# A two-layer streaming-encoder trunk: a rebuilt prologue, three pairs of weight slabs multiplied tile by tile, the low weight halves made in quarters, rotations in two banks

## The reference

```python
mod = (c @ w + b)                      # adaLN: 1024 x 3072 matrix, per layer and sub-layer
shift, scale, gate = split(mod, 3)
u = x * (1 + scale) + shift
# mixer
proj = u @ w_in                        # split into a, g (conv group), q, k, v (attention group)
h = silu(layer_norm(causal_dwconv(a * sigmoid(g), conv_w (31 taps), conv_b)))
q, k = partial_rotary(q, cos, sin), partial_rotary(k, cos, sin)   # angles = positions * inv_freq
o = swa_sink_attention(q, k, v, sinks) # chunks of 64 frames, window 128
y = concat([h, o]) @ w_out
x = layer_norm(DN_ALPHA * x + (1 + gate) * y)
# MLP, with its own adaLN
val, g = split(u @ w_up)               # D_FF = 2816
y = (val * silu(causal_dwconv(g, 3 taps))) @ w_down
x = layer_norm(DN_ALPHA * x + (1 + gate) * y)
```

## Time and profile before

| | |
|---|---|
| median of three runs | 2279.89 us |
| the profiled execution: its own time | 2280.07 us |
| its span, first to last instruction | 2278.3 us |
| TensorE busy | 2131.2 us (94%) |
| VectorE, ScalarE, GpSimd busy | 1255.8, 1008.8, 1230.0 us |
| mean granted TensorE clock | 0.971 |
| w_lo on GpSimd (L1506) | 392 instructions, 858.2 us |
| waits of TensorE, largest | 26.6 us for first_acc, 19.7 us for the parameter rows |

### The profile page before, as it was taken

The page is one execution under the profiler, slowest core; times in us unless marked ns, Lnnn a source line. Parts: engine busy times, 40 slices in busy tenths (PEclk is TensorE's granted clock), DMA queues, the critical chain, the costliest instruction groups (busy, mean ns, idle before and its releaser), DMA issues.

```text
span 2278.3 us, 25841 instructions
## 1 busy us (share of the span) xinstructions
PE 2131.2 (94%) x9491; PEld 1717.9 (75%) x9491; DVE 1255.8 (55%) x1924; ACT 1008.8 (44%) x1758; POOL 1230.0 (54%) x702
## 2 busy tenths in 40 slices
...
GB/s 247 133 137 131 37 163 96 98 124 141 114 127 102 110 120 134 134 152 113 88 73 94 102 91 98 95 96 84 85 80 88 100 83 102 111 94 129 93 95 72
DMA packets 414058, 248.72 MB, mean 109 GB/s; under 512 B 44293, under 2 KB 389101, under 8 KB 412909
## 3 DMA queue, kind: packets, MB, share of 16 engines
...
q10 hardware_dynamic: 2221, 0.55, 0.1%
...
## 4 chain that ended last, share of the span: by engine, by line
PE 74%; DVE 9%; POOL 7%; issue 5%; ACT 3%; DMA 1%; ACTq 0%; DVEq 0%; POOLq 0%
PE fg L699 23%; PE fg L701 23%; PE fg L700 23%; POOL w_lo L1506 2%; POOL ada_acc L1550 2%; DVE bank_c L1209 1%; DVE st L1325 1%; PE bank_s L767 1%; DVE probs L1329 1%; POOL ssum L1557 1%; DMA rows<-in_ffn_conv_w_dram 1%; DVE first_acc L1150 1%; ACT tmp L885 1%; POOL q L1535 0%; PE bank_t L776 0%
## 5 line engine op out<-in xcount | busy, mean ns | idle before, releaser
L1506 POOL TENSOR_TENSOR w_lo<-raw,w_hi 128x1024 fp32r<-128x1024 f32 (+2 forms) x392 | 858.2, 2189 | 932.3 <-ACT w_hi L877 932.1
L699 PE MATMUL fg<-u_hi,w_hi 128*128 128x512 f32 x2112 | 856.0, 405 | 14.6 <-DVE u_lo L1189 6.3
L700 PE MATMUL fg<-u_lo,w_hi 128*128 128x512 f32 x2112 | 829.2, 393 | 0.0
L701 PE MATMUL fg<-u_hi,w_lo 128*128 128x512 f32 x2112 | 828.9, 392 | 0.0
L877 ACT ACTIVATE w_hi<-raw 128x1024 fp32r<-128x1024 f32 (+2 forms) x392 | 379.4, 968 | 409.3 <-PE fg L701 349.2
L699 PEld LDWEIGHTS fg<-u_hi,w_hi 128*128 128x128 f32 x2112 | 401.2, 190 | 120.9 <-issue 22.9
L700 PEld LDWEIGHTS fg<-u_lo,w_hi 128*128 128x128 f32 x2112 | 401.1, 190 | 89.8 <-issue 10.3
L701 PEld LDWEIGHTS fg<-u_hi,w_lo 128*128 128x128 f32 x2112 | 400.4, 190 | 86.0
L1430 DVE SCALAR_TENSOR_TENSOR x<-fg,mod,x 128x512 f32<-128x512 f32 x160 | 119.8, 749 | 347.7 <-PE fg L701 347.7
L1209 DVE SCALAR_TENSOR_TENSOR bank_c<-glu,par,bank_c 128x512 f32<-128x512 f32 x448 | 306.1, 748 | 0.0
L699 PE MATMUL fg<-h_hi,w_hi 128*128 128x512 f32 x704 | 281.7, 400 | 0.2 <-DVE h_lo L1463 0.2
...
## 6 DMA issues: line engine op xcount, KB each, us to landing
raw<-in_w_up_dram SPq DMA_DIRECT2D x176, 512.0 KB, 3.8
...
```

The source lines that it names most:

```text
L699: pe.matmul(out[:], hi[:, k, :], rhi, start=k == order[0], stop=False)
L700: pe.matmul(out[:], hi[:, k, :], rlo, start=False, stop=False)
L701: ins = pe.matmul(out[:], lo[:, k, :], rhi, start=False, stop=k == order[-1])
L1506: pool.tensor_tensor(w_lo[n % NRAW][:, 0:nk, :], raw[n % NRAW][:, 0:nk, :], w_hi[n % NHI][:, 0:nk, :].bitcast(F32), ALU.subtract).then_inc ...
```

## The change

1. **Prologue.** The first adaLN matrix comes in eight pieces of 512 rows by 512 columns (four column chunks, two pieces each), each with a buffer of its own, laid between the loads of x. VectorE adds up chunk by chunk, TensorE sums a chunk over partitions as soon as it is complete, straight into `bank_s`, from which VectorE folds `gain` and `bias`. The angles go to GpSimd, the conv weights' rows and the sinks are loaded later, ScalarE alone empties the banks of x, and slabs 0 and 1 are both split before. VectorE makes its own copy of the modulated input (`first_tmp`) while ScalarE writes `u_hi` from x.
2. **Pairs.** Slabs 0 and 1, 22 and 23, 36 and 37 are multiplied together: for each tile of the input the three matmuls of one slab, then the three of the other. Both have to be ready at the start.
3. **Quarters.** GpSimd makes `w_lo` two tiles (256 columns) at a time.
4. **Rotations** alternate between `bank_t` and `bank_s`.
5. **Plan.** `u_lo` of block 1 moves from VectorE to GpSimd and costs the planner nothing, so that taps move to earlier slots; the eight squares of the first residual norm stand in one slot, its other steps one slot earlier, and its last step (`xo`, ScalarE) in slots 38 to 45; adaLN chunks 11 to 23 come later.

```diff
-    fixed = {... "xl": 7, "il": 10, "xt": 7, ...}
+    fixed = {... "xl": 7, "il": 0, "xt": 7, ...}
+PAIRS = (0, POS["o", 0, 0, 0], FIRST_UP)
-    x_norm(0, wait + 9, 4, wait + 12, wait + 13, 4)
+    x_norm(0, wait + 9, 8, wait + 11, wait + 12, 4)
+    for k in range(DT):
+        put(wait + 17 + k, "xo", 0, k)
...
@@ SyncE
             def load_first(k):
-                if k >= 3:
-                    sp.wait_ge(first_add, k - 2)
-                sp.dma_start(first_ada[k % 3][:], a["w_ada_mix"][0, k * P:(k + 1) * P, 0:2 * D]).then_inc(in_first[k % 3], 16)
+                rows, cols = slice(k % 2 * D // 2, (k % 2 + 1) * D // 2), slice(k // 2 * T, (k // 2 + 1) * T)
+                sp.dma_start(first_ada[k][:], a["w_ada_mix"][0, rows, cols].rearrange("(k p) n -> p k n", p=P)).then_inc(in_first[k], 16)
-            for t in range(TB):
-                load_x(t)
-            for k in range(6):
-                load_first(k)
-            load_w(0)
-            load_first(6)
-            load_first(7)
+            load_x(0)
+            load_first(0)
+            for t in range(1, TB):
+                load_x(t)
+                load_first(t)
+            load_first(4)
+            load_w(0)
+            load_first(5)
+            load_first(6)
+            load_first(7)
+            load_w(1)
+            load_rows(rows2, rows3)
...
@@ TensorE
+            def slabs(*ns):
...
+                    for n in ns:
+                        out, hi, lo = fg[BANK[n]], w_hi[n % NHI], w_lo[n % NRAW]
+                        pe.matmul(out[:], hi[:, k, :], rhi, start=k == order[0], stop=False)
+                        pe.matmul(out[:], hi[:, k, :], rlo, start=False, stop=False)
+                        ins = pe.matmul(out[:], lo[:, k, :], rhi, start=False, stop=k == order[-1])
...
-                take("t", rope_add, (QT + 2) * mi + (j + 1 if j < QT else QT + 2))
-                pe.matmul(bank_t[:], rot, q[mi][:, :, j, :] if j < QT else k_raw,
+                take("ts"[j % 2], rope_add, (QT + 2) * mi + (j + 1 if j < QT else QT + 2))
+                pe.matmul((bank_t, bank_s)[j % 2][:], rot, q[mi][:, :, j, :] if j < QT else k_raw,
...
+            for c in range(CHUNKS_BEFORE):
+                pe.wait_ge(first_add, DT * (c + 1))
+                for i in range(c * TB, (c + 1) * TB):
+                    ins = pe.matmul(bank_s[:, i:i + 1], first_acc[:, i * P:(i + 1) * P], ones_1[:, 0:1], start=True, stop=True)
...
@@ VectorE
+            for c in range(CHUNKS_BEFORE):
+                for k in range(DT):
+                    add_first(c, k)
+            fold("ss", 0)
...
+                first_tmp(k)
+                if k:
+                    first_lo(k - 1)
...
@@ GpSimd
-                pool.tensor_tensor(w_lo[n % NRAW][:, 0:nk, :], raw[n % NRAW][:, 0:nk, :], w_hi[n % NHI][:, 0:nk, :].bitcast(F32),
-                                   ALU.subtract).then_inc(lo_ready, 1)
+                for k in range(0, nk, LO_TILES):
+                    ks = slice(k, min(k + LO_TILES, nk))
+                    ins = pool.tensor_tensor(w_lo[n % NRAW][:, ks, :], raw[n % NRAW][:, ks, :], w_hi[n % NHI][:, ks, :].bitcast(F32),
+                                             ALU.subtract)
+                ins.then_inc(lo_ready, 1)
...
+            def second_lo(k):
+                pool.wait_ge(ihi, DT + k + 1)
+                pool.tensor_tensor(u_lo[1][:, k, :], tmp[:, k % 2, :], u_hi[1][:, k, :].bitcast(F32), ALU.subtract).then_inc(ilo, 1)
...
+            angles()
+            pool.wait_ge(first_add, DT * CHUNKS_BEFORE)
+            for n in range(2):
+                split_lo(n)
```

More of the change, by code:

```diff
@@ L63 @@
     _n += _c
-IN_CONST = 2 + len(ROWS1) + 2 * DEPTH
+IN_CONST = 1 + len(ROWS1)
 def conv_slabs(l, b, tiles):
```

346 lines of the change are left out of this document (183 added, 163 removed).

## The result

| | before | after |
|---|---|---|
| median, us | 2278.94 (2276.76 to 2280.75, 4 runs) | 2229.89 (2227.96 to 2231.71, 4 runs) |
| ratio | | 0.9781, 95% interval 0.9768 to 0.9793 |
| profiled execution, us | 2280.07, span 2278.3 | 2230.16, span 2228.4 |
| GpSimd busy, us | 1230.0 (54%) | 1422.8 (64%) |
| VectorE busy, us | 1255.8 | 1183.0 |

The change wins 50 us, and 2230 was forecast. The total hides that it is made of other parts than I had said. The first view to read is the windows by stage, cut at the starts of the slabs that bound the stages (core, then per engine busy us and count, granted clock, DMA share, GB/s); they answer to the earlier trace rows.

The account below looks back on a forecast made before the run. TensorE was taken as nearly always busy from 700 us, so gains lay in the first 430 us: 24.5 + 5.5 + 5.4 + 10.5 + 6.5 = 52.4 off 2280.07, taken as 50: 2230 us, 8-in-10 range 2214 to 2252.

Parts of the forecast that it names:

- A: Prologue and first pair: first matmul at 45 us, slab 2 at 59 instead of 83.2, gain 24 us (14 to 27).
- B: Slabs 2 to 13: GpSimd becomes the bound, first scores at 150 to 154; 24.5 us gained together with the prologue.
- G: The rest of the kernel: extra GpSimd pieces against shorter VectorE waits, counted 0, from -4 to +4 us.
- E: First residual norm and third pair, 337 to 393 us: earlier scale and filled wait, gain 10.5 us (6 to 13).
- F: Rotations of block 1, 393 to 428 us: two banks leave one wait of 2.6 us, gain 6.5 (3 to 8).
- D: Behind slab 21: taps moved ahead leave only the last sum, gain 5.4 us; second pair booked at 0.
- C: Slots 14 to 21: quarters shorten VectorE's waits for GpSimd, gain 5.5 us, bounds 0 and 10.
- rival (3): Quarters free VectorE more widely, in slots 14 to 21 and beats behind 428 us: 8 us more, about 2221; chance 0.13.
- 1 (0.9 us a piece): GpSimd swallows more: w_lo pieces cost 0.9 us instead of 0.69, 14 to 16 us less gain, 2245; chance 0.2.
- 2 (transfers): Prologue bound by its transfers at 300 GB/s, last piece 8 us later, 2239 to 2242 us; chance 0.12.
- 4: Slower than before: w_lo pieces have a floor of about 1.2 us, some 70 slots lose, 2290 to 2350; chance 0.03.
- 5: A new wait, such as pairs needing both w_lo, eats the first stage: same time within 0.2%; chance 0.02.

Follow-up runs that it names:

- e3_nopairs: The changed kernel with no slab pairs; 2221.38 us, ratio 0.9742 to the kernel before.
- e1_whole: The changed kernel with w_lo in one whole 128x1024 piece per slab again; 2235.53 us, ratio 0.9805 to the kernel before.
- e10_both: The changed kernel with only the first pair, the cosine product ahead of w_lo (mixers 1 to 3), whole w_lo in slabs 0-16 and 110-140; 2205.21 us.
- e12_ulo: e10_both with the eight u_lo of block 1 computed on VectorE again instead of GpSimd; 2210.32 us, ratio 0.9687 to the kernel before.
- e4_onebank: The changed kernel with all rotations in bank_t, as before; 2243.01 us, ratio 0.9836 to the kernel before.
- e6_bank: The changed kernel, all three pairs, with banks 1 and 2 exchanged from slab 36 on; 2222.26 us, ratio 0.9753 to the kernel before.
- e2_quarters: The kernel before with one edit, w_lo in pieces of two weight tiles; 2267.71 us, ratio 0.9945 to the kernel before.
- e7_product: The changed kernel with the first pair alone and GpSimd's cosine product ahead of w_lo for mixers 1 to 3; 2210.78 us, ratio 0.9699 to before.
- e9_adaplaces: The kernel before with only the change's places of the adaLN quarters and their folds; 2278.41 us, ratio 0.9992 to the kernel before.

## Why the prediction was right, step by step

The total is right, and by luck: A and B gave 3.6 us more than forecast and G 12, E and F 13.7 less, D and the slabs from 22 to 33 4.4 less. A and C hold in the main, B and D in part; E, F and G miss.

**A, 24 forecast, 25.6 measured.** VectorE's last seven adds ended at 37.0, the last sums took 1.86 us, the two folds 0.17 each, the eight pieces of `w_lo` 6.51 for my 5.5 and five VectorE instructions of 0.55 between them, 8.3 in all, and the first matmul came at 43.9 for 45 (answers to the earlier trace rows):

```profile
31.51 5.54 DVE L1173 SCALAR_TENSOR_TENSOR first_acc<-first_ada,ccol,first_acc 128x512 f32<-128x512 f32 x7
37.11 1.86 PE L846 MATMUL bank_s<-const,first_acc 128*128 128x1 f32 x8 [4.17 <-DVE first_acc L1173]
37.19 6.51 POOL L1533 TENSOR_TENSOR w_lo<-raw,w_hi 128x256 fp32r<-128x256 f32 x8 [3.12 <-issue]
43.91 0.77 PE L727 MATMUL fg<-u_hi,w_hi 128*128 128x512 f32 x1 [4.20 <-POOL w_lo L1533]
```

The last piece of the matrix landed at 33.4 us for my 33. The middle of the prologue moved 373 GB/s (16 to 28 us) for my 390, but VectorE waited for no piece behind 27.9 us, so its adds set the end and not the transfers. The 28 steps of the angles took 18.4 us on GpSimd (15.7 to 34.1), not my 12: about 0.66 us each for my 0.4, and they ended only 3 us ahead of the last add. Of the 25.6 us at slab 2 the pair is 3.2: it starts 1.6 us later than slab 0 alone does in `e3_nopairs`, since it needs two `w_lo`, and more than makes up for it. No run takes the rest of the prologue apart.

**B, 24.5 with A, 28.1 measured.** First scores at 150.1, the edge of my 150 to 154, with GpSimd busy 98% of 77 to 150 us. The number is right; the reason is only half so. `e1_whole` and `e10_both` show that the price of the pieces there is 3.6 and 2.6 us, and `e12_ulo` that relieving GpSimd of 9 us there buys nothing, so that it was not the bound alone. `e4_onebank` adds that 7 us of this stage's gain are the two rotation banks', which I had priced only in F, and 8.4 us of TensorE's time went at its end into the wait for `kz`.

**C, 5.5 forecast, 5.6 measured** (28.1 at the first scores and at slab 15, 33.7 at slab 21). `e1_whole` puts the value of quarters from slab 15 to 21 at 7.6. L1357 fell below half its mean (383 against 1538 ns), L1349 did not (297 against 394).

**D, 5.4 forecast, 3.8 measured** from slab 21 to 22. Behind the second pair the gain is 5.4 larger (4 of it the pair's, by `e3_nopairs`) and GpSimd takes it back, as booked; but it takes more: the gain falls from 42.9 to 34.7 us at slab 33. A `w_lo` in slots 22 to 29 costs 2.82 us, and with one sum and two adds a slab needs 6.7 us. I had six slots at 0.4 us and the pair's gain; slabs 24 to 30 lost 5.8 us, which is about that, and then slab 33 lost 2.4 more, behind six sums of squares (8.46 us in one run of GpSimd's timeline) that now stand together ahead of the next `w_lo`. TensorE waited 2.0 us for the first residual total, not 8 to 10, and that total came at 299.4, not near the 287 that I had named as a sign. That sign didn't fit my own sum: before, the total came at 336.5, and 24.5, 5.5 and 5.4 us less is 301.

**E, 10.5 forecast, 4.8 from slab 33 to 38 and 2.4 from slab 30 on.** This is the first of the steps that failed. I wrote "the pair starts when v has left its bank", gave it 33 us after the total and 11 us of matmuls. The total (`ssum`) ended at 299.4; the pair started 40.8 us later and took 13.4, since TensorE had rested and the clock stood at 0.51. I saw the wait for the bank and did not ask what stands ahead of that copy in ScalarE's queue, nor what three engines do while two gates come out together. `e6_bank` shows the price of the bank, 7.6 us. And the pair was not needed for the 10.5: from slab 33 to 38 the gain is 11.7 us with no pairs, 9.1 with the first alone and 10.2 with all three and the bank free. Quarters of `w_lo` alone give 0.1 there (`e2_quarters`), so it must come from the plan's edits, the squares in one slot, the later `xo` and adaLN chunks; no run takes these apart.

**F, 6.5 forecast, -1.5 measured.** The gain is 4.9 us from slab 38 to 42, and then 6.3 are given back up to slab 44. I wrote that "one wait of 2.6 us stays". It is 4.6 us for `kz`. The step's error is that it counted sums of rotation j - 2 and not the last product, which stood behind a `w_lo` before as well. With one bank the wait is all but hidden behind the waits for the bank (9.6 us for q, 1.3 for `kz` in `e4_onebank`): slabs 42 to 44 take 13.6 us there, in the changed kernel 19.4, and in `e7_product` 12.1. With the product first, F is 9.3 us.

**G, 0 forecast, +12 measured.** The mechanism was named as a rival (3): beats behind 428 us are the same code as those of C. I gave it 4 us. From slab 44 to 84 it is 16.7. With quarters alone these slabs gain 12.1 us, without quarters but with all else 11.2; so each lifts the same jam, and neither share is the whole. In before, the four L1276 of slots 69 to 79 mean 1778 ns, in after 952; before:

```profile
L1276 DVE SCALAR_TENSOR_TENSOR tmp<-tmp,conv 128x512 f32<-128x512 f32 x4 | 7.1, 1778 | 0.0
L1325 DVE TENSOR_TENSOR st<-st 128x4 f32<-128x4 f32 x4 | 6.8, 1692 | 0.0
```
after:
```profile
L1308 DVE SCALAR_TENSOR_TENSOR tmp<-tmp,conv 128x512 f32<-128x512 f32 x4 | 3.8, 952 | 0.0
L1357 DVE TENSOR_TENSOR st<-st 128x4 f32<-128x4 f32 x4 | 1.6, 412 | 0.0
```

Then 4.6 us are given back from slab 115 to 133; whole pieces win 4.2 there, so most of it is the quarters' price in the slots of the norm and of the adaLN adds, the 1 to 2 us I had named, and larger.

**The rivals.** 1 (0.9 us a piece): a piece costs 0.70 back to back (2.80 for four), its mean is 0.765; not so. 2 (transfers): 299 GB/s over the whole prologue, but 373 in its middle, and the last piece landed at 33.4 us, not 8 us later; not so. 3: in part. The gain behind 428 us is there with three times its size, but C gave 5.6 and not 10, and without the quarters 7 of G's 12 us stay. 4 and 5: not so as a whole, though 5's words, that a pair brings a new wait, are true of the third pair.

What stays open: what each edit of the prologue gave of the 20.0 us at slab 0, and each of the plan's edits in E; whether the 8.4 us of waiting for `kz` in block 0 go when its product comes first; why `e9_adaplaces` differs from execution to execution, and how the 11 us of the jam at slots 69 to 79 divide between the places of the adaLN quarters and the order ahead of them.
